# Both merge gates of a hybrid decoder layer as seven block products per chunk

## Reference

```python
u = _rmsnorm(h, mix_pre_g[l])
c_q, c_kv, k_rope_raw, xb, yb, gate_mla, gate_lru = jnp.split(u @ w_in[l], split_points, axis=-1)
o_mla = _mla_branch(...)   # latent attention, 8 heads
o_lru = _rglru_branch(xb, yb, ...)
merged = jax.nn.sigmoid(gate_mla) * o_mla + jax.nn.sigmoid(gate_lru) * o_lru
h = h + _rmsnorm(merged @ w_out[l], mix_post_g[l])

def _rglru_branch(xb, yb, conv_w, conv_b, w_rg, b_rg, w_ig, b_ig, lru_lambda, w_o_lru):
    xc = conv_b + sum(xpad[:, k:k + s] * conv_w[k] for k in range(CONV_WIDTH))
    r, ig = sigmoid(block-diagonal products of xc)
    a = jnp.exp(log_a)
    gated_x = jnp.sqrt(-jnp.expm1(2.0 * log_a)) * (ig * xc)
    _, h = lax.associative_scan(_lru_combine, (a, gated_x), axis=1)
    return (h * jax.nn.gelu(yb)) @ w_o_lru
```

## Time and profile before

| | us |
|---|---|
| median of 3 runs | 2288.66 (2287.89 to 2289.98) |
| the profiled execution, whole | 2287.68 |
| its span, first to last instruction | 2285.9 |
| PE busy | 2154.8 |
| DVE busy | 1387.9 |
| ACT busy | 975.1 |
| POOL busy | 450.0 |

### The profile page before, as it was taken

One profiled execution on the slowest core, in us unless ns is written; L12 is line 12 of the kernel. 1 busy time (PEld: TensorE's weight loads), 2 busy tenths in 40 slices (PEclk: granted clock), 3 DMA queues, 4 the chain that ended last, 5 costly groups with the idle time before them and its releaser, 6 DMA issues.

```text
span 2285.9 us, 25908 instructions
## 1 busy us (share of the span) xinstructions
PE 2154.8 (94%) x9837; PEld 1788.0 (78%) x9837; DVE 1387.9 (61%) x1718; ACT 975.1 (43%) x1543; POOL 450.0 (20%) x453
## 2 busy tenths in 40 slices
PE   4999999999998999999999888998599999999997
PEld 3888788878886888888888777777488888888885
DVE  7668865557575656211213788677756766557666
ACT  5333333334353776311323666445433333334343
POOL 5123320000032221000012555215312321000012
PEclk8999999999999999999999999999799999999998
DMA  3345442252442221222410100455135453216334
GB/s 120 93 155 187 155 168 69 70 198 96 154 148 78 52 52 49 74 65 77 119 43 23 29 15 10 161 194 175 55 96 188 168 192 124 72 51 221 101 134 143
DMA packets 220294, 249.85 MB, mean 109 GB/s; under 512 B 24262, under 2 KB 161547, under 8 KB 220171
## 3 DMA queue, kind: packets, MB, share of 16 engines
q1 hardware_dynamic: 220170, 248.19, 33.3%
HBM read 192.06 MB, written 55.57 MB: 108 GB/s over the span
## 4 chain that ended last, share of the span: by engine, by line
PE 86%; DVE 6%; ACT 3%; POOL 3%; issue 2%; DMA 1%; POOLq 0%; SPq 0%; ACTq 0%; DVEq 0%
PE ps L88 28%; PE ps L90 28%; PE ps L89 28%; PE ps L2172 1%; PE ps L2140 1%; POOL a_rot L2057 1%; PE ps L357 1%; ACT a_probs L2116 1%; DVE a_pt L98 1%; DVE ff_t L98 1%; DVE a_s L2106 0%; DVE entry_y L342 0%; DVE w_lo L98 0%; DMA w_raw<-in_w_out_dram 0%; ACT entry_squares L282 0%
## 5 line engine op out<-in xcount | busy, mean ns | idle before, releaser
L98 DVE TENSOR_TENSOR ff_w_lo<-ff_raw,ff_w_hi 128x512 fp32r<-128x512 f32 x264 | 210.9, 802 | 171.9 <-ACT ff_w_hi L94 171.7
L88 PE MATMUL ps<-ff_t,ff_w_hi 128*128 128x512 f32 x704 | 275.5, 391 | 15.8 <-DVE ff_t L98 15.8
L89 PE MATMUL ps<-ff_t,ff_w_hi 128*128 128x512 f32 x704 | 275.1, 391 | 0.0
L90 PE MATMUL ps<-ff_t,ff_w_lo 128*128 128x512 f32 x704 | 275.1, 391 | 0.0
L94 ACT ACTIVATE ff_w_hi<-ff_raw 128x512 fp32r<-128x512 f32 x264 | 164.8, 628 | 180.4 <-PE ps L90 174.9
L88 PE MATMUL ps<-d_b_hi,d_a_hi 128*128 128x512 f32 x608 | 237.6, 391 | 3.7 <-DVE d_a_lo L98 3.7
L98 DVE TENSOR_TENSOR w_lo<-w_raw,w_hi 128x1024 fp32r<-128x1024 f32 (+2 forms) x81 | 93.6, 1160 | 237.4 <-ACT w_hi L94 237.3
L90 PE MATMUL ps<-d_b_hi,d_a_lo 128*128 128x512 f32 x608 | 236.8, 390 | 0.0
L89 PE MATMUL ps<-d_b_lo,d_a_hi 128*128 128x512 f32 x608 | 236.8, 389 | 0.0
L88 PE MATMUL ps<-ff_b,ff_w_hi 128*128 128x512 f32 x528 | 209.0, 396 | 13.5 <-issue 8.3
L89 PE MATMUL ps<-ff_b,ff_w_hi 128*128 128x512 f32 x528 | 207.8, 394 | 0.0
(11 more groups left out here) (296 smaller groups left out, 4362.4 us busy)
## 6 DMA issues: line engine op xcount, KB each, us to landing
ff_raw<-in_ffn_w_gate_dram SPq DMA_DIRECT2D x44, 512.0 KB, 3.9
ff_raw<-in_ffn_w_up_dram SPq DMA_DIRECT2D x44, 512.0 KB, 4.0
d_sums<-in_ffn_w_down_dram SPq DMA_DIRECT2D x44, 512.0 KB, 4.1
sums_scratch<-d_sums SPq DMA_DIRECT2D x88, 256.0 KB, 2.6
w_raw<-in_w_in_dram SPq DMA_DIRECT2D x32, 512.0 KB, 3.9
d_raw<-sums_scratch SPq DMA_DIRECT2D x24, 512.0 KB, 3.3
w_raw<-in_w_out_dram SPq DMA_DIRECT2D x24, 512.0 KB, 4.3
spill_scratch<-ff_st SPq DMA_DIRECT2D x44, 256.0 KB, 2.6
```

What stands on the lines that cost most here:

```text
L88: pe.matmul(out, lh, rh, start=start, stop=False, skip_group_check=go_on)
L89: pe.matmul(out, lh, rl, start=False, stop=False, skip_group_check=go_on)
L90: return pe.matmul(out, ll, rh, start=False, stop=stop, skip_group_check=go_on)
L98: return nc.vector.tensor_tensor(lo, src, as_f32(hi), ALU.subtract)
```

## The change

Both gates (2048 columns of `w_in`) leave stages 2 and 3 and form a stage of their own between the recurrence and the latents, class `MergeGates`. For each m of 8, two 128-column blocks (m % 4 and m % 4 + 4 of one gate) are computed with seven products of 12 matmuls each, in the order `G_ORDER`: (0,1), (0,2), (0,6), (0,7), (0,5), (1,1), (1,2), (0,3), (0,4), ... Products 1, 2, 3 use u; 5, 6, 7, 4 use combinations of u's four blocks, kept in `g_t` (64 KB per partition, 16 places of high and low part). Product 6 is added in PSUM to 1, 5 to that and 3 to that, with a snapshot by ACT (`snap`) before each next one; DVE adds products 2, 7 and 4 (`cadd`) into the snapshots, ACT takes four sigmoids, and SP stores them to DRAM for both gates. DVE forms four sums of weight blocks per m (`sums`), ACT and DVE split seven weight operands of 512 columns into four slots.

The combinations are formed in four groups inside the recurrence: POOL after its products of blocks 1 to 4 (`t_wholes`, `t_sums`), split by ACT (`t_hi`) and DVE (`t_lo`); a last one by DVE after the recurrence (`t_last`). Since `g_t` takes the place of `lru_hi` and `lru_lo`, each result of the recurrence is stored to DRAM (`keep`) and read back after the latents, through the raw buffers, into the place of u (`row_hi`, `row_lo`). `convolve(d)` waits for the store of d - 2. The branch products with `w_o_lru` now follow the latents and values, before the units; the last chunk's are put between the units (`last_lows`, `last_highs`), and the sigmoids of their gate are loaded back. The diff, cut:

```diff
+    def keep(self, sp, d):
+
+        sp.wait_ge(self.S["out_done"], d + 1)
+        sp.dma_start(self.kept[d * P:(d + 1) * P, :], self.xc[:, d % 2, :]).then_inc(self.c.f.d_in[2 + d % 2], 16)
+
+    def wait_kept(self, eng, d):
+        eng.wait_ge(self.c.f.d_in[2 + d % 2], 16 * (STEPS // 4 + d // 2 + 1))
...
+    def t_wholes(self, pool, k):
+
+        c, v = self.c, self.nc.gpsimd
+        if k == 0:
+            pool.wait_ge(c.norm.by["u_split"], 2 * NT)
+            c.norm.all_stored(pool, NT)
+        v.tensor_tensor(self.blocks(k, 0, 2, 0, True), as_f32(self.halves(c.u_hi, k)), as_f32(self.halves(c.u_lo, k)), ALU.add)\
+            .then_inc(self.S["t_sum"], 1)
+        if k < 3:
+            v.tensor_tensor(self.blocks(k, 2, 2, 0, True), as_f32(self.halves(c.u_hi, 4 + k)), as_f32(self.halves(c.u_lo, 4 + k)),
+                            ALU.add).then_inc(self.S["t_sum"], 1)
+        else:
+            cols = half_of(1)
+            v.tensor_tensor(self.t_raw[:, 8 + k, 0, :], as_f32(c.u_hi[:, 4 + k, cols]), as_f32(c.u_lo[:, 4 + k, cols]), ALU.add)\
+                .then_inc(self.S["t_sum"], 1)
+
+    def t_sums(self, pool, k):
+
+        v, n = self.nc.gpsimd, 6 * k
+        h11, h12, h21, h22 = (self.t_raw[:, 4 * b + k, 0, :] for b in ((0, 1, 2, 3) if k < 3 else (0, 1, 1, 2)))
+        t1, t2, t3, t4 = (self.t_raw[:, 4 * b + k, 1, :] for b in range(4))
+        pool.wait_ge(self.S["t_sum"], n + 2)
+        v.tensor_tensor(t1, h12, h11, ALU.subtract).then_inc(self.S["t_sum"], 1)
+        v.tensor_tensor(t3, h22, h12, ALU.subtract).then_inc(self.S["t_sum"], 1)
+        pool.wait_ge(self.S["t_sum"], n + 3)
+        v.tensor_tensor(t2, h22, t1, ALU.subtract).then_inc(self.S["t_sum"], 1)
+        if k < 3:
+            pool.wait_ge(self.S["t_sum"], n + 5)
...
+    def t_last(self, dve):
+
+        c, v, n, cols = self.c, self.nc.vector, 23, half_of(0)
+        h, t = self.t_raw[:, 15, 0, :], self.t_raw[:, 15, 1, :]
+        dve.wait_ge(self.rec.S["out_done"], DK)
+        dve.wait_ge(self.S["t_sum"], n)
+        v.tensor_tensor(h, as_f32(c.u_hi[:, 7, cols]), as_f32(c.u_lo[:, 7, cols]), ALU.add).then_inc(self.S["t_sum"], 1)
+        v.tensor_tensor(t, as_f32(self.t[:, 7, 0, :]), as_f32(self.t[:, 7, 1, :]), ALU.add).then_inc(self.S["t_sum"], 1)
...
+    def t_hi(self, act, k):
+        count = 4 if k < 3 else 3
+        act.wait_ge(self.S["t_sum"], 6 * (k + 1) if k < 3 else 23)
+        split_hi(self.nc, self.blocks(k, 0, count, 0), self.blocks(k, 0, count, 1, True)).then_inc(self.S["t_hi"], 1)
+
+    def t_lo(self, dve, k):
+        count = 4 if k < 3 else 3
+        dve.wait_ge(self.S["t_hi"], k + 1)
+        split_lo(self.nc, self.blocks(k, 0, count, 1), self.blocks(k, 0, count, 1, True), self.blocks(k, 0, count, 0))\
+            .then_inc(self.S["t_lo"], 1)
...
+    def snap(self, act, m, p):
+        c, F, block, S = self.c, self.c.f, self.SNAP_TO[p], self.rec.S
+        act.wait_ge(F.prod, self.at(m, p) + 1)
+        if p == 1 and m >= 2:
+            act.wait_ge(self.S["stored"], 32 * (m - 1))
+        elif p == 1 and m == 1:
+            self.rec.wait_kept(act, DK - 2)
+        elif p == 1:
+            act.wait_ge(S["out_done"], DK - 1)
+        elif p == 6 and m == 1:
+            act.wait_ge(S["m_done"], DK)
+        self.nc.scalar.activation(self.partial(m, block), c.ps[:, self.banks(m)[0], :], ACT.Copy).then_inc(F.snap[p], 1)
...
+    def sums(self, dve, m):
+        F, v, n = self.c.f, self.nc.vector, 4 * (self.nm(m) - 1)
+        a, b = self.raw_of(m, 0), self.raw_of(m, 1)
+        a11, a12, a21, a22, s1 = a[:, 0:HALF], a[:, HALF:SEQ], b[:, 0:HALF], b[:, HALF:SEQ], self.s1[:, :]
+        self.raw_landed(dve, m, 1)
+        if m > 0:
+            dve.wait_ge(F.w_lo, self.at(m - 1, 5) + 1)
+        else:
+            self.w.wait_done(dve, self.rec.n_y[DK - 1])
+        v.tensor_tensor(s1, a21, a22, ALU.add).then_inc(F.sums, 1)
+        v.tensor_tensor(a21, a11, a21, ALU.subtract).then_inc(F.sums, 1)
+        dve.wait_ge(F.sums, n + 2)
+        v.tensor_tensor(a11, s1, a11, ALU.subtract).then_inc(F.sums, 1)
+        dve.wait_ge(F.sums, n + 3)
+        v.tensor_tensor(a12, a12, a11, ALU.subtract).then_inc(F.sums, 1)
...
+    def product(self, pe, m, p):
+        c, F, S = self.c, self.c.f, self.rec.S
+        self.wait_split(pe, m, p)
+        if p == 1:
+            if m >= 2:
+                pe.wait_ge(self.S["sig"], self.n_sig(m - 2, 12))
+            elif m == 0:
+                pe.wait_ge(S["conv_done"], DK)
+                pe.wait_ge(S["gelu_done"], DK)
+            else:
+                pe.wait_ge(S["sig_i"], DK)
+        if p == 2 and m >= 2:
+            pe.wait_ge(F.cadd[2], self.nm(m) - 2)
+        if p == 6:
+            pe.wait_ge(F.snap[1], self.nm(m))
+            if m == 0:
+                pe.wait_ge(self.S["t_lo"], 4)
...
+                    if d + 2 < DK:
+                        w.hi(act, rec.n_x[d + 2])
+                    elif d + 2 == DK:
+                        gates.hi(act, 0, 1)
+                        gates.hi(act, 0, 2)
+                    else:
+                        gates.hi(act, 0, 6)
+                        gates.hi(act, 0, 7)
                     rec.sigmoids(act, d)
                     if d + 1 < DK:
                         rec.gates_hi(act, d + 1)
                         rec.conv_hi(act, d + 1)
                     rec.decay(act, d)
                     rec.root(act, d)
-                    if d + 2 <= DK:
-                        w.hi(act, (rec.n_y + [ring[1]])[d + 2])
+                    if d + 2 < DK:
+                        w.hi(act, rec.n_y[d + 2])
                     if d + 1 < DK:
                         rec.gelu(act, d + 1)
-                    rec.out_hi(act, d)
-
-                for at, n in enumerate(ring):
-                    if at + 3 < len(ring):
-                        w.hi(act, ring[at + 3])
-                    elif at + 3 < len(ring) + 2:
-                        w.hi(act, lat.n_g[at + 3 - len(ring)])
-                    if n in lru.n_g:
-                        lru.sigmoid(act, lru.n_g.index(n))
+                    if 1 <= d <= 4:
+                        gates.t_hi(act, d - 1)
...
                     rec.products(pool, d)
+                    if 1 <= d <= 4:
+                        gates.t_wholes(pool, d - 1)
+                        gates.t_sums(pool, d - 1)
                 lat.blank(pool)
                 for s in range(NT):
                     lat.rstd_of(pool, s)
                     if s == 4:
                         lat.rotate(pool, 0)
+                lat.rotate(pool, 1)
+                att.rope_pool(pool, units[0])
+                att.rope_pool(pool, units[2])
                 att.blank(pool)
...
+                    if d + 2 < DK:
+                        w.lo(dve, rec.n_x[d + 2])
+                    elif d + 2 == DK:
+                        gates.lo(dve, 0, 1)
+                        gates.lo(dve, 0, 2)
+                    else:
+                        gates.sums(dve, 0)
+                        gates.lo(dve, 0, 6)
+                        gates.lo(dve, 0, 7)
+                    if 2 <= d <= 5:
+                        gates.t_lo(dve, d - 2)
...
+                for m, p in G_ORDER:
+                    gates.product(pe, m, p)
                 lat.project(pe, 0)
-                lat.project(pe, 1)
-                lat.turn(pe, 0)
-                for s in range(2, NT):
-                    lat.gate_of(pe, s)
+                for s in range(1, NT):
...
     def blank(self, pool):
-        pool.wait_ge(self.lat.S["proj_done"], NT)
+        self.wait_unit(pool, self.units[0])
+        self.merge.all_stored(pool)
```

633 lines of the change are left out of this document (407 added, 226 removed).

## The result

The changed kernel takes 2339.7 us (median of four runs, 2338.1 to 2342.5) against 2288.7 us for the kernel before on the same chip: ratio 1.0224, 95% interval 1.0206 to 1.0241. The forecast was 2336.6, its range 2290 to 2352.

What follows compares the result with a forecast made beforehand. TensorE was taken to bound the kernel, at 0.2267 us per recurrence gate matmul. Terms 36.6 + 2.1 + 2.9 + 0.7 + 6.6 = +48.9 on 2287.7 gave 2336.6 us, range 2290 to 2352.

Steps and rivals of the forecast that it cites:

- B: End of GpSimd's second product in a recurrence block, after which the scan can start; for block 6 forecast 45 us later.
- Part 1: Gate products on TensorE: 96 fewer matmuls save 21.8 us.
- Part 2: Recurrence: GpSimd's six sums enter the loop to the next convolution, moving block 6 by 45 us; the large term.
- The choice at the ports: Recurrence: VectorE and GpSimd take turns with start-ups overlapped, sums done after 14.3 us; whole durations would give 15.1.
- Part 3: Start of the gates: TensorE waits for the first snapshot; +36.6 us including both earlier terms, then +2.1 for second snapshot and clock.
- part 4: Latents: weight rows loaded late, +2.9 us; values: a split queued behind rows of the recurrence, +0.7 us.
- part 5: Entry to the attention: six clears wait for the last branch product's store, directly ahead of the first normalising; +6.6 us.
- The signs: Expected in the profile after: convolutions 36 to 37 us apart, six additions over 12 to 16, TensorE below 75% busy.
- (a): Recurrence: VectorE and GpSimd don't hinder each other, so GpSimd needs 10.4 instead of 14.3 us; 2321 us, 12%.
- (b): Slow recurrence blocks: TensorE's clock stays at 1.2 GHz, some 38 us more; 2375 us, 8%.
- (c): Recurrence: the sums fit into GpSimd's idle time, the loop stays at 24.5 us; 2291.6 us, 10%.
- (d): Whole kernel: only the saved matmuls count, every wait hidden and clears off the chain; 2266 us, 5%.

Runs made afterwards that it cites:

- run two: Changed kernel with `t_hi` a block later, and GpSimd's sums split between its two products and behind VectorE's product with the gelu: 2300.2 us.
- Run three: Changed kernel with GpSimd's sums cut to 8 of each 512 columns, full-size splits reading `u_hi`, combinations not computed: 2306.2 us.
- run four: Changed kernel with GpSimd waiting for VectorE's product with the gelu ahead of all six sums: 2341.7 us.
- runs five: Changed kernel with the last block reordered: sigmoids first, then the snapshot of (0,1) and splits ahead, VectorE's order to match: 2337.8 us.
- eight: Changed kernel with sums in GpSimd's gaps, early snapshot and spread clears, plus VectorE's weight sums and additions placed earlier: 2286.0 us.
- nine: Kernel of run eight with the first pair of sigmoid buffers exchanged, so the snapshot of (0,1) gets another place, and some splits and additions reordered: 2283.8 us.
- run six: Changed kernel with the six clears of `a_q` and `a_k` one by one behind GpSimd's attention steps 0 to 5: 2333.4 us.
- run one: Changed kernel with `t_hi` one block later and `t_lo` one block later ahead of `mix`, GpSimd's sums left in place: 2311.7 us.

## Why the prediction was right, point by point

| term | predicted | measured |
|---|---|---|
| six sums done, from B | 14.3 | 13.8 |
| next convolution, from B | 20.6 | 20.05 |
| cycle of a block with four sums of 512 | 36.6 | 36.0 |
| cycle of the last group | 33.2 | 32.6 |
| cycle free of sums | 24.0 | 24.8 |
| B of block 6 moved by | 45 | 45.0 |
| snapshot ends, from B of block 6 | 19.0 | 18.5 |
| first matmul of the latents | 1118.7 | 1119.8 |
| waits in the latents | 2.9 | 2.1 |
| wait at the values | 3.0 | 3.0 |
| from the end of unit 3 to the first transpose | 14.7 | 14.1 |
| first transpose moved by | 48.9 | 50.6 |

**Part 1** held. Between 969.3 and 1119.8 stand 54 products: 146.9 us at the pitch of the earlier trace rows, and 150.4 measured, 3.5 more, of which I can place the low clock at the start (2.35 us over the first 11 matmuls, 4.83 against 11 x 0.2267) and 0.78 us at one snapshot.

**Part 2** held, the large term with it. The sum of the five cycles from block 1 to block 6 came out 43.6 us longer, and block 1 itself was 1.4 later than before. The 45 is thus right partly by accident: the ports cost 0.6 us a block less than I put, while block 1 was late and the cycle free of sums is 0.8 us longer. From the end of the product to that convolution it is 4.3 us (930.57 to 934.84), not the 3.7 that I took from a store of the same size. In the changed kernel this wait counts in that one cycle; in run two, where it is 3.9 to 4.4 us, it bounds the recurrence.

The order at the ports was not the one that I put. I had the scan first and the four 512-column additions alone behind everything; the first addition went ahead of the scan (785.41 against 785.49), and two of the four took 2.16 and 2.27 us, where 1.3 was my sign. The total doesn't depend on the order, so the 14.3 was safe from this error.

The choice at the ports, 14.3 by turns with overlapped start-ups against 15.1 by the rule of the Trainium skill ("SBUF — State Buffer", section "SBUF: two separate sides"), came out on the side of the rows, 13.8. Run three shows that the rule is right in what it says, one engine waits for the other's whole instruction, even with 16 columns of its own. The 15.1 was too high for two reasons. Its five gaps of 0.08 us between additions aren't there: run four has the six additions in 10.0 us and, with VectorE's three ahead of them, everything in 14.6. And at each of six changes of turn 0.1 to 0.2 us overlap, 0.8 in all, which makes 13.8.

**Part 3** held in its sum and was incomplete in its reading. The snapshot was the wait that ended last, 18.5 us behind B of block 6. Directly behind it stood VectorE's weight sums and additions; that took runs five, eight and nine to see. The prediction didn't need it, since it asked for the first wait only.

**Parts 4 and 5** held to 1.3 and 0.6 us: 50.6 us later than before at the first transpose with 48.9 predicted. From the first matmul of the latents to the end of unit 3 it takes 177.4 us (1119.76 to 1297.16), where before 172.5 are left for the same work (1252.5 - 1080.0): 4.9 more, with 3.6 put. The waits that part 4 names account for 2.8 of it (2.1 + 3.0 against 2.3). I can't place the other 2.1, but for a granted clock of 0.80 to 0.86 between 1125 and 1135 us. From there to the first transpose it is 14.1 us with 14.7 put: 4.7 until the product with the last gate is done (4.6 put), 2.8 for its store (3.7 put), 5.5 for the clears, 1.1 for the first normalising. Before it was 8.1, so part 5 measured 6.0 for 6.6. Only 4.6 of this go when the clears are spread (run six): in the same 14.1 us TensorE also waits 4.3 us for that last product ahead of its second scores, a wait that part 5 doesn't name and that the clears covered.

**After that** the profiled execution loses more, which no term has: attention step 63 is 52.0 us late where step 8 was 49.9, and the second FFN begins 54.2 late. This execution was 2.8 us above the median of its four. The last 2.2 us are hardly its own: from step 63 to the second FFN it is 183.5 us here and 183.1 to 183.8 in eight of the nine runs, against 181.4 before; run one, with 181.5, is the exception. The cause isn't known.

**The signs.** Convolutions 36.0 us apart, six additions over 13.8 us, one idle time of 11.4 us ahead of the first `g_t` matmul and TensorE full for 150 us from there are as named. ScalarE idles 13.0 us before `g_t`, not 8 to 12. TensorE is busy 75.2% between 810 and 970, where I had named less than 75. The first 1024-column addition took 2.40 us and not more; the second took 4.38.

**The rivals.** (a) needed GpSimd's sums at their own speed: run four and the 4.47 us scan exclude it. (b): the clock did fall, to 0.90 on average over 800 to 1000, but the loop that set the time has no TensorE in it except for the gates, and from a convolution to the end of GpSimd's second product it took 16.0 us as before (805.50 to 821.48). TensorE then waited 4.1 to 6.5 us for each convolution, so its clock decided nothing there. (c): `t_hi` waited 13 us, the sums didn't fit ahead of `w_hi`; they do fit in GpSimd's idle time when split in two and with `t_hi` a block later (run two, 2300.2). (d), 2266, fell: no version came below 2283.8.

## What to carry to other kernels

An engine that is busy 20% of the time has room for more work only at the places where nobody waits behind it: with the same instructions the kernel took 2339.7 us, 2311.7 when ScalarE no longer waited for GpSimd's additions in the loop, and 2300.2 when the additions also stood in two of GpSimd's idle times. When a wait is to be removed, list what comes second at the same place before pricing it; here two edits at the start of the gates gave 2.3 of 11 and 1.8 of 4 us, because the next wait lay close behind, and the one that took up the next waits too gave 6.8 of 9.5. And in these runs two-operand instructions of VectorE and GpSimd that read SBUF added up, at 1024, 512 and 16 columns, so a short one beside a scan was no short one.

## What the runs showed of the hardware beyond what I expected

- An addition of 16 columns on GpSimd took 0.21 us alone and 2.19 us when VectorE's scan had begun 0.11 us before it. An addition of 1024 columns took 2.40 when it began 0.08 us before the scan, and 4.38 when it began during it.
- VectorE's convolution, which reads PSUM and one operand in SBUF, did not hold GpSimd: in run one GpSimd's first product took 2.40 us beside it (from 826.52, the convolution's last three instructions from 826.17 in 3.92 us, as in the earlier trace rows).
- TensorE's clock: after 11.37 us of idle, matmuls were 0.427 us apart up to 974.15 (1.2 GHz; 0.56 after the very first, 969.32), then 0.227: 4.8 us at the low level. After the 5.93 us of the earlier trace rows it was 4.3 us. Twice the idle time hardly lengthened the recovery.
